# Gated delta rule in a one-core kernel: scalar-engine groups of four per-head pieces, issued with or without a wait on the piece in front

## What is computed

```python
def step(S, inp):
    qc, kc, vc, gc, bc = inp
    gc = jnp.cumsum(gc, axis=-1)
    decay = jnp.exp(jnp.where(incl, gc[..., :, None] - gc[..., None, :], -jnp.inf))
    kk = jnp.einsum('bhid,bhjd->bhij', kc, kc)
    a = eye + jnp.where(strict, kk * decay * bc[..., :, None], 0.0)
    rhs = jnp.concatenate([vc * bc[..., None], kc * (bc * jnp.exp(gc))[..., None]], axis=-1)
    sol = lax.linalg.triangular_solve(a, rhs, left_side=True, lower=True, unit_diagonal=True)
    u, w = sol[..., :dv], sol[..., dv:]
    v_new = u - jnp.einsum('bhcd,bhde->bhce', w, S)
    qk = jnp.where(incl, jnp.einsum('bhid,bhjd->bhij', qc, kc) * decay, 0.0)
    o = (jnp.einsum('bhcd,bhde->bhce', qc * jnp.exp(gc)[..., None], S)
         + jnp.einsum('bhij,bhje->bhie', qk, v_new))
    S = (S * jnp.exp(g_last)[..., None]
         + jnp.einsum('bhcd,bhce->bhde', kc * jnp.exp(g_last - gc)[..., None], v_new))
    return S, o
```

## Time and profile before

| | us |
|---|---|
| median of 3 runs | 4279.09 |
| lowest, highest | 4276.19, 4282.10 |
| profiled execution, first to last instruction (span) | 4275.4 |
| PE busy in it | 3506.1 |
| DVE busy | 2659.6 |
| ACT busy | 1401.6 |
| POOL busy | 1205.5 |

### The profile page before, as it was taken

The page is one execution under the profiler, slowest core; times in us unless marked ns, Lnnn a source line. Parts: engine busy times, 40 slices in busy tenths (PEclk is TensorE's granted clock), DMA queues, the critical chain, the costliest instruction groups (busy, mean ns, idle before and its releaser), DMA issues.

```text
span 4275.4 us, 38801 instructions
## 1 busy us (share of the span) xinstructions
PE 3506.1 (82%) x11382; PEld 1852.2 (43%) x11382; DVE 2659.6 (62%) x5456; ACT 1401.6 (33%) x3747; POOL 1205.5 (28%) x1228
## 2 busy tenths in 40 slices
PE   7888978999867677779998987877788787877877
PEld 3334436844335555567554542322233256322222
DVE  3656455849656666633779658777555455887444
ACT  1232120004524544441333333433433221433333
POOL 0001100001005444520333433433434201434432
PEclk9889989999989998989999999999999998999999
DMA  5523324645321111043899999999999723999998
GB/s 215 197 79 136 121 85 165 224 165 189 138 71 33 52 52 57 17 166 143 349 415 397 406 409 421 403 422 421 409 417 413 326 79 142 413 421 414 417 421 360
DMA packets 169764, 1088.28 MB, mean 255 GB/s; under 512 B 16432, under 2 KB 45488, under 8 KB 51152
## 3 DMA queue, kind: packets, MB, share of 16 engines
q0 software_dynamic: 112608, 820.04, 46.7%
q1 hardware_dynamic: 56944, 265.77, 16.9%
HBM read 1075.19 MB, written 10.55 MB: 254 GB/s over the span
## 4 chain that ended last, share of the span: by engine, by line
PE 34%; DVE 24%; DMA 18%; issue 12%; POOL 7%; ACT 6%; DVEq 0%; SPq 0%; POOLq 0%; ACTq 0%
PE bank L199 19%; DMA arena<-in_uv,arena 15%; POOL arena L3018 6%; DVE arena L3035 6%; ACT arena L211 5%; PE bank L2986 4%; DVE arena L443 2%; PE bank L1620 2%; DVE arena L561 2%; PE bank L2454 2%; DVE arena L217 1%; PE bank L2151 1%; PE bank L2143 1%; DVE arena L221 1%; DMA arena<-in_w_rows 1%
## 5 line engine op out<-in xcount | busy, mean ns | idle before, releaser
L2986 PE MATMUL bank<-arena 128*128 128x512 f32 x3072 | 1486.8, 618 | 355.0 <-ACT arena L211 352.2
L211 ACT ACTIVATE arena<-arena 128x1 f32<-128x1 f32 (+4 forms) x2831 | 949.6, 335 | 2005.7 <-DVE arena L3035 1123.7
L199 PE MATMUL bank<-arena 128*128 128x256 f32 (+4 forms) x4640 | 1298.6, 439 | 69.8 <-ACT arena L211 35.3
L3035 DVE CUSTOM_DVE_ANT_0 arena<-arena 128x1024 f32<-128x1024 f32 x768 | 941.8, 1226 | 607.2 <-DMA arena<-in_uv,arena 568.9
L3018 POOL DMA_INDIRECT arena<-in_uv,arena x768 | 791.0, 1030 | 1254.2 <-PE bank L2986 856.7
L2986 PEld LDWEIGHTS bank<-arena 128*128 128x128 f32 x3072 | 544.5, 191 | 1269.9 <-ACT arena L211 825.4
L199 PEld LDWEIGHTS bank<-arena 128*128 128x128 f32 (+2 forms) x4640 | 805.1, 196 | 551.9 <-issue 424.2
L211 ACT ACTIVATE arena<-bank 128x512 f32<-128x512 f32 (+4 forms) x306 | 160.8, 525 | 496.5 <-PE bank L199 318.6
L443 DVE CUSTOM_DVE_ANT_0 arena<-arena 128x1024 f32<-128x1024 f32 x192 | 241.2, 1256 | 33.5 <-DMA arena<-in_w_rows 21.9
L211 ACT ACTIVATE arena<-bank,arena 128x128 f32<-128x128 f32 (+1 forms) x400 | 162.4, 406 | 286.8 <-PE bank L2143 224.2
L626 POOL TENSOR_SCALAR arena<-arena 128x1 f32<-128x1 f32 (+3 forms) x48 | 16.2, 337 | 665.2 <-ACT arena L211 471.0
(11 more groups left out here) (251 smaller groups left out, 2493.4 us busy)
## 6 DMA issues: line engine op xcount, KB each, us to landing
arena<-in_w_rows SPq DMA_DIRECT2D x50, 1024.0 KB, 5.0
arena<-in_w_in SPq DMA_DIRECT2D x16, 2048.0 KB, 8.0
arena<-in_wq SPq DMA_DIRECT2D x14, 2048.0 KB, 8.5
arena<-in_dn_w SPq DMA_DIRECT2D x12, 2048.0 KB, 10.0
arena<-in_w_up SPq DMA_DIRECT2D x11, 2048.0 KB, 7.9
arena<-in_dn_wo SPq DMA_DIRECT2D x8, 2048.0 KB, 11.3
arena<-in_w_rows POOLq DMA_DIRECT2D x14, 1024.0 KB, 5.7
arena<-decay_rest SPq DMA_DIRECT2D x56, 256.0 KB, 5.0
```

Source lines behind the costliest of these rows:

```text
L199: t = p.e.matmul(out, l, r, start=(i == 0), stop=(i == n - 1))
L211: return a().activation(out, in_, f, **kw)
L2986: t = p.e.matmul(by[half], m["dg"][ee % 4], m["uv"][r][:, 1024 + 512 * half:1536 + 512 * half], start=(ee == 0), stop=(ee == 127))
L3035: v().tensor_tensor_reduce(self.spare, uv[:, 0:1024], m["ht"][n % 2], 1.0, 0.0, ALU.mult, ALU.add, m["acts"][:, ee:ee + 1]).then_inc(*V.up ...
```

## The change

In three places the first piece of a group of four is issued through the wrapper as before, and the second to fourth through the bare engine, without the wait on the piece in front. The arguments, the order and the counts (`then_inc`) are the same. The instruction after a group still waits for the fourth piece.

```diff
@@ act_prep, round 0
                     for h in range(4):
-                        t = act(a, x[:, H4[h]], x[:, H4[h]], ACT.Identity, bias=m["GC"][:, d, c, 4 * g + h:4 * g + h + 1], scale=-1.0)
+                        t = (a() if h == 0 else a.e).activation(x[:, H4[h]], x[:, H4[h]], ACT.Identity,
+                                                               bias=m["GC"][:, d, c, 4 * g + h:4 * g + h + 1], scale=-1.0)
                         t.then_inc(*(self.A.up("pr.d", k, d) if h == 3 else self.A.up("pr.dh")))
@@ act_inverse, part 1 of each level
                 for h in range(4):
-                    t = act(a, m["T"][:, H4[h]], self.banks.at("in.y", k, l)[:, H4[h]], ACT.Copy,
-                            scale=m["BS"][:, n, c, 4 * g + h:4 * g + h + 1])
+                    t = (a() if h == 0 else a.e).activation(m["T"][:, H4[h]], self.banks.at("in.y", k, l)[:, H4[h]], ACT.Copy,
+                                                           scale=m["BS"][:, n, c, 4 * g + h:4 * g + h + 1])
                     t.then_inc(*(A.up("in.T", k, l) if h == 3 else A.up("in.Th")))
@@ act_scaled (keys re.E2 and re.Sg)
         for h in range(4):
-            t = act(a, out[:, H4[h]], x[:, H4[h]], ACT.Copy, scale=by[:, h:h + 1])
+            t = (a() if h == 0 else a.e).activation(out[:, H4[h]], x[:, H4[h]], ACT.Copy, scale=by[:, h:h + 1])
             t.then_inc(*(self.A.up(key, k, d) if h == 3 else self.A.up(key + "h")))
```

## The result

The changed kernel takes **4250.9 us** (median of 5, 4248.8 to 4257.0), the kernel before 4280.9 in the same comparison (5 runs, 4276.2 to 4283.0). The ratio is 0.9936, with a 95% interval of 0.9925 to 0.9948: 22 to 32 us less. Predicted were 4256 us with a range of 4246 to 4266, and faster with 0.85.

What follows compares the result with a forecast made beforehand. The latency of ACT's groups of four was taken to bound the stage: 66 groups x 0.378 = 24.9 us, less 2, is 23 us. 4275.4 becomes 4252.4; with the median's 3.7 us offset 4256 us, range 4246 to 4266.

Steps and rivals of the forecast that it cites:

- What bounds the stage: Inverse loop through the engines: latency of a group of four pieces, not ACT's load, is on the path.
- The price of a wait: ACT's groups of four: a removed wait is worth 0.033 + 0.093 = 0.126 us, a group 0.38 us.
- the pair in the earlier trace: ACT activation with accumulator, then its reading without a wait: overlap 0.093 us taken; 0.11 with a PSUM source.
- The high end: ACT's groups: pieces follow at the column streaming rate; a removed wait is worth 0.29 us, a group 0.88.
- (c): ACT's groups: fetch of the scale column hidden too, a group saves 0.65 us; 4239 us, chance 0.05.
- The low end (a): ACT's groups: only empty time between pieces goes, 0.10 us per group, 6.5 us; 4273 us, chance 0.08.
- rival (b): ACT's groups: nothing goes, the 0.033 us is needed between any two instructions; groups 1.57 us, 4279 us, chance 0.04.
- How many groups: Chain from 1248 to 1870 us: 66 of 136 groups lie on it, 66 x 0.378 = 24.9 us.
- What is late next: Before each T, PE's earlier work; idle times fit the cut but one; 2 us lost in all, leaving 23 us.
- The stretch where ACT is the chain: T group starting at 1429.13 will wait for its bank: 0.3 us lost, about 1 us with two repetitions.
- What follows the stage: in_dn_w waits and everything behind the recurrence: nothing tied to an earlier moment, so 23 us reach the end undiminished.
- rival (d): PE granted the lower clock in more places, about 2 us each, deciding from 12; 4320 us with 32, chance 0.03.

Runs made afterwards that it cites:

- The inverse alone: Kernel before with only the 64 groups of the inverse (in.T) issued without inner waits: 4257.6 us against 4277.6, ratio 0.9945.
- the preparations: Kernel before with only the 32 groups of act_prep issued without inner waits: 4276.2 us against 4277.6, ratio 0.9993.
- an edit whose own part in the stage is some 5 us by the estimate: Inner waits removed from DVE's 24 recurrence groups: on the changed kernel 4238.5 us (4250.9 without), on the kernel before 4275.6 against 4278.7.

## Why the prediction was right, point by point

- **What bounds the stage.** Right: the latency of groups of four in the loop through the engines. The inverse alone gave 20 of the 27 to 30 us, the preparations nothing that can be measured.
- **The price of a wait.** Too low: 0.126 us predicted, 0.14 measured (0.43 / 3). I took the overlap of the pair in the earlier trace rows, which reads SBUF, for all groups and set aside the one in the earlier trace rows, which reads PSUM, as being of a wider shape. Each has proved about right for its own source: the groups that read SBUF overlap by 0.09 us, those that read a bank by 0.11, and 56 of the 66 on the chain read a bank. The high end is excluded: a group takes 1.14 us, where it would have been 0.69, and 0.92 if the fetch of the scale column were hidden (c). The low end (a) and rival (b) fall with the same row.
- **How many groups.** 66 x 0.43 = 28 us is the most that the chain of before can give back. By kind: 46 T groups on the chain x 0.43 = 20 us, and 20.0 measured; 18 groups of `act_scaled` x 0.43 = 8, and 11.9 measured; two preparations 0.8, and 1.4 measured. That the first agrees to the decimal is luck, with an interval of 18 to 29.5 us. The count is borne out as far as 5 us can be seen.
- **What is late next.** This was the weak step. I looked at PE's idle times before each T and found them all longer than the cut, and gave 2 us for the rest. What came up was not PE's own work but others of its waits: for DVE's substitution, 43.3 to 51.2 us, and for its subtraction, 8.6 to 13.1. My rows had the first of them, as the second entry of the earlier trace rows, and the text did not speak of it. In the profiles the stage became 21.0 to 26.9 us shorter, depending on which is set against which, so 1 to 7 us of the 28 were lost where I had 2.
- **The stretch where ACT is the chain.** Right: its T group now waits for the bank, 0.51 us where I had 0.3.
- **What follows the stage.** Right: 2393.2 us before and after. The three transfers of `in_dn_w` on the chain have kept their length (31.8 us together before, 31.5 after), though PE's waits for them have not, 30.3 to 28.1 us.
- **The clock, rival (d).** It needed twelve more drops. The two profiles of the change have three at a place where the first profile of before has none and the second has one, 1.8 us each in the rows shown, and lack others, as the one at 1343 us. The granted clock over the stage shows no loss, 0.911 and 0.915 after 0.919 and 0.911.
- **The sum.** The profile of the change has a span of 4255.2 us where I had 4252.4, so there the saving was 3 us less than forecast. The median lies 4.3 us below that span, where in the kernel before it lay 3.7 above its own, which I took over: the offset was a matter of which execution had been profiled. This is why the median, 4251, is 5 us better than the 4256 predicted while the profile is 3 us worse.

So the mechanism was right, and that the number came so near was in part luck: the price was 3 us too low, the loss to other waits was up to 5 us more than the 2 I had, which goes the other way, and the offset of the median was off by 8. The forecast of 23 us is inside the interval of 22 to 32, and how the last 5 us divide is not shown.

## What to carry to other kernels

An engine's wait on its own instruction in front costs the overlap and a short gap, here 0.13 to 0.14 us each, on ACT and DVE alike; drop it where neighbours touch different data and the group is part of a loop through several engines, and expect nothing where the engine is waiting for another one anyway. Count the groups on the chain of waits, not those in the program: 32 groups, all but two of them off it, gave nothing that could be measured. Before giving a number for the remainder, read the second entry of the list of waits as well as the first, since that is what the gain will run into. And before a few microseconds between two profiles are put down to an edit, compare the granted clock of the stage in both: here an edit whose own part in the stage is some 5 us by the estimate gave 12 in one kernel and 3 in another.

## What the runs showed of the hardware

**DVE instructions with two inputs in SBUF are held up beside POOL's large ones; those with one input in PSUM are not.** In the profile of the change, one stretch of the substitution:

```profile
1463.83 1.68 POOL L627 TENSOR_TENSOR arena<-arena 128x8 f32<-128x8 f32 x1
...
1464.89 0.22 DVE L2112 TENSOR_TENSOR arena<-arena 128x56 f32<-128x56 f32 x1
...
1465.65 2.22 POOL L2262 TENSOR_TENSOR arena<-arena 128x512 f32<-128x512 f32 x2
1465.86 0.89 DVE L2112 TENSOR_TENSOR arena<-arena 128x40 f32<-128x40 f32 x1
...
1466.78 0.19 DVE L2110 TENSOR_TENSOR arena<-bank,arena 128x32 f32<-128x32 f32 x1
1467.00 0.92 DVE L2112 TENSOR_TENSOR arena<-arena 128x32 f32<-128x32 f32 x1
```

The largest of these, in front of POOL's two of 128x512 and beside a POOL instruction of 128x8, takes 0.22 us; two smaller ones beside the large two take 0.89 and 0.92, and the one between these, which has an input in a bank, 0.19. Over the whole stage the 128x40 ones take 0.86 to 1.27 us beside POOL's large instructions (7 of 16) and 0.20 otherwise (9 of 16), those of the same width with an input in a bank 0.20 always. Not every one beside a large instruction is held up: of the 128x56 ones beside them the shortest takes 0.22. This agrees with the Trainium skill (SBUF — State Buffer, "Who interferes with whom"), which has it that a vector instruction with two SBUF inputs contends with a GpSimd instruction that reads SBUF, and one with at most one SBUF input does not. Adding up what DVE's instructions take above the shortest of their kind, on the chain alone, gives 22.5 us in the kernel before and 38.1 in the changed one, nearly all of it beside POOL's large instructions: 16 of the 38 us by which DVE's share of the chain rose. The prediction did not have it, and it may be why a strand on DVE does not get shorter evenly when something in front of it does; no run here leaves POOL's instructions out to show it.

**The granted clock of PE differs between executions of the same kernel** at the same place: 1.00 and 0.66 in the windows above, for 3.4 us. Over the 14 profiles what stands before the stage took 1246.6 to 1251.5 us and what stands behind it 2392.5 to 2396.5, although no kernel changed either. Single executions of the kernel before lay between 4270 and 4285 us. Differences of 5 us between two kernels are therefore open here, even with five runs each.
